# Sums of squares by head of the first attention, from high and low parts

## The reference, cut to what matters

```python
q = l2_norm(q) * (A_HEAD_DIM ** -0.5)      # x * rsqrt(sum(x*x, -1) + EPS), 16 heads of 128
k = l2_norm(k)
...
lower = where(tri_strict, einsum('bhncd,bhnsd->bhncs', k_beta, k) * decay, 0.0)
sol = triangular_solve(eye + lower, rhs)
qk = einsum('bhncd,bhnsd->bhncs', q, k) * decay
...
o = rms_norm_2(o, out_norm_w)              # over the 128 channels of a head
```

## Time and profile before

| what | us |
|---|---|
| median of 3 runs | 1421.38 (1419.54 to 1422.17) |
| the profiled execution's own time | 1419.68 |
| its span in the trace | 1417.9 |
| PE busy | 1391.6 (98%) |
| weight loads busy | 1186.7 (84%) |
| DVE busy | 974.6 (69%) |
| ACT busy | 763.8 (54%) |
| POOL busy | 142.5 (10%) |

### The profile page before, as it was taken

How to read it: one execution, slowest core, us unless ns; L and a number is a source line. 1 busy time by engine, 2 the same in 40 slices (tenths; PEclk the granted TensorE clock), 3 DMA queues, 4 the chain that set the end, 5 groups by cost and what they waited for, 6 DMA issues and landing times.

```text
span 1417.9 us, 20634 instructions
## 1 busy us (share of the span) xinstructions
PE 1391.6 (98%) x7982; PEld 1186.7 (84%) x7982; DVE 974.6 (69%) x1199; ACT 763.8 (54%) x923; POOL 142.5 (10%) x148
## 2 busy tenths in 40 slices
PE   6999999999999999999899999999999999999998
PEld 2446999888888888888799988888888888888887
DVE  3748999876678787789856748746655666656552
ACT  2215435455686677743456665546556566556431
POOL 0000011000060321011234300000000000000000
PEclk9999999999999999999999999999999999999999
DMA  9998899764365445463544566544545555555552
GB/s 385 417 412 349 332 409 409 250 204 152 134 238 192 157 171 182 161 215 136 184 160 144 183 196 215 183 169 171 201 148 188 184 178 178 180 176 179 177 188 81
DMA packets 78295, 303.72 MB, mean 214 GB/s; under 512 B 8768, under 2 KB 8896, under 8 KB 73728
## 3 DMA queue, kind: packets, MB, share of 16 engines
q1 hardware_dynamic: 67680, 261.30, 51.8%
q0 software_dynamic: 10528, 41.19, 8.2%
HBM read 291.97 MB, written 12.58 MB: 215 GB/s over the span
## 4 chain that ended last, share of the span: by engine, by line
PE 87%; DVE 7%; DMA 2%; ACT 2%; issue 1%; SPq 1%; DVEq 0%
PE acc L729 36%; PE acc L731 18%; PE misc L756 3%; PE acc L756 3%; DVE w_lo L1579 3%; PE misc L985 2%; PE acc L687 2%; PE acc L688 2%; PE acc L689 2%; PE acc L679 2%; PE acc L678 2%; PE acc L676 2%; DMA mod_ring<-mod_w 1%; PE misc L880 1%; PE misc L679 1%
## 5 line engine op out<-in xcount | busy, mean ns | idle before, releaser
L1579 DVE TENSOR_TENSOR w_lo<-raw,w_hi 128x1024 fp32r<-128x1024 f32 x392 | 478.1, 1239 | 247.2 <-ACT w_hi L1151 242.5
L729 PE MATMUL acc<-b_op,w_hi 128*128 128x512 f32 x1792 | 635.1, 398 | 2.6 <-DVE vo L1617 2.3
L1151 ACT ACTIVATE w_hi<-raw 128x1024 fp32r<-128x1024 f32 x392 | 405.7, 1054 | 262.5 <-PE acc L731 145.8
L731 PE MATMUL acc<-b_op,w_lo 128*128 128x256 f32 x1792 | 499.4, 279 | 0.0
L729 PEld LDWEIGHTS acc<-b_op,w_hi 128*128 128x128 f32 x1792 | 336.3, 188 | 79.6 <-DVE vo L1617 2.6
L731 PEld LDWEIGHTS acc<-b_op,w_lo 128*128 128x128 f32 x1792 | 337.6, 188 | 0.5
L729 PE MATMUL acc<-a_op,w_hi 128*128 128x512 f32 x768 | 269.0, 396 | 0.5 <-DVEq L1968 0.5
L731 PE MATMUL acc<-a_op,w_lo 128*128 128x256 f32 x768 | 213.7, 278 | 0.0
L729 PEld LDWEIGHTS acc<-a_op,w_hi 128*128 128x128 f32 x768 | 144.1, 188 | 34.9 <-DVEq L1968 0.8
L731 PEld LDWEIGHTS acc<-a_op,w_lo 128*128 128x128 f32 x768 | 144.5, 188 | 0.1
L1549 DVE CUSTOM_DVE_ANT_0 mod_ring<-mod_ring,silu_b,vecs 128x2048 f32<-128x2048 f32 x26 | 61.1, 2351 | 46.9 <-DMA mod_ring<-mod_w 46.7
(11 more groups left out here) (251 smaller groups left out, 1845.3 us busy)
## 6 DMA issues: line engine op xcount, KB each, us to landing
raw<-weights SPq DMA_DIRECT2D x392, 512.0 KB, 4.2
mod_ring<-mod_w SPq DMA_DIRECT2D x26, 1024.0 KB, 12.7
u_ring<-weights SPq DMA_DIRECT2D x32, 512.0 KB, 13.0
gate_ring<-weights POOLq DMA_DIRECT2D x30, 512.0 KB, 8.4
mod_late<-mod_w SPq DMA_DIRECT2D x6, 1024.0 KB, 6.3
xres<-x_t SPq DMA_DIRECT2D x4, 512.0 KB, 15.5
xres<-x_t POOLq DMA_DIRECT2D x4, 512.0 KB, 8.6
x_d<-xres POOLq DMA_DIRECT2D x1, 2048.0 KB, 9.1
```

The source lines that it names most:

```text
L729: nc.tensor.matmul(to, w_hi[:, slot, ch], op[:, kt], start=kt == 0, stop=False, skip_group_check=True)
L731: last = nc.tensor.matmul(to[:, 0:T], w_lo[:, slot, ch], op[:, kt, 0:T], start=False, stop=kt == KT - 1, skip_group_check=True)
L1151: nc.scalar.activation(w_hi[:, m.c % HL_SLOTS], raw[:, q.c % RAW_SLOTS], ACT.Copy).then_inc(own.up(s_hi), 1)
L1579: nc.vector.tensor_tensor(w_lo[:, slot], raw[:, q.c % RAW_SLOTS], w_hi[:, slot].bitcast(F32), ALU.subtract).then_inc(own.up(s_lo), 1)
```

## The change

Eleven of the twelve calls of `head_sums` (all but the last sum of o) become sums from two fp32r parts.

- ACT: `norm_inputs` gets a copy of the squares in t2 to `qk_hi` behind the square; behind the squares of o in t4, for j = 0 to 2, there is a copy to `o_hi[j]`. Both raise `s_heads_hi`. The copy of ones to `ones_r` moves from behind the first attention to the start of its loop.
- DVE: `heads_low(n, lo, src, hi)` waits for `s_heads_hi`, subtracts in place (the low part lies where the squares were) and raises `s_heads_lo`. For the query sums it stands behind `query_products` and ahead of `lo_parts(n + 2, 2)`, in round 0 behind these; for the key sums between the first and the second of five `lo_parts`; for o behind the second slab of a group's eight.
- PE: `qk_sums(c)` and `o_sums(j)` wait for `s_heads_lo` and run `sums_of_parts`, two fp32r matmuls a head, at the places where `head_sums` was called.

```diff
--- before.py
+++ after.py
@@ -241,6 +241,7 @@
         t0_at = top[0]
         t0 = at("t0", [P, 8 * REACH], F32)
         t1 = at("t1", [P, 4 * T], F32)
+        t2_at = top[0]
         t2 = at("t2", [P, 4 * T], F32)
         t34_at = top[0]
         t3 = at("t3", [P, 4 * T], F32)
@@ -309,6 +310,10 @@
         sq_hi = at("sq_hi", [P, 4 * T], F32R, vo_at)
         sq_lo = at("sq_lo", [P, 4 * T], F32R, vo_at + 16 * T)
         v_n = at("v_n", [P, 2, GC], F32, vo_at + 8 * PAIRS)
+        t2_lo = at("t2_lo", [P, 4 * T], F32R, t2_at)
+        t4_lo = at("t4_lo", [P, 4 * T], F32R, t34_at + 16 * T)
+        qk_hi = at("qk_hi", [P, 4 * T], F32R, vo_at + 32 * T)
+        o_hi = [at(f"o_hi{j}", [P, 4 * T], F32R, a_at + o) for j, o in enumerate((8192, 8192, 16384))]
         k_s = at("k_s", [P, 4 * T], F32, vo_at + 32 * T)
         acc = ctx.enter_context(nc.psum_tensor("acc", [P, 2, 4 * T], F32))
         misc = ctx.enter_context(nc.psum_tensor("misc", [P, 2048], F32))
@@ -431,6 +436,8 @@
         s_zs = sem("s_zs")
 
         s_ones = sem("s_ones")
+        s_heads_hi = sem("s_heads_hi")
+        s_heads_lo = sem("s_heads_lo")
         s_sqh = sem("s_sqh")
         s_sql = sem("s_sql")
         s_bx = sem("s_bx")
@@ -892,21 +899,35 @@
                                             start=True, stop=True)
                 last.then_inc(s_nrm, 1)
 
+            def sums_of_parts(hi, lo, at_):
+
+                for h in range(BATCH):
+                    out, of = misc[:, at_ + h * T:at_ + (h + 1) * T], slice(h * T, (h + 1) * T)
+                    nc.tensor.matmul(out, ones_r[:], hi[:, of], start=True, stop=False)
+                    last = nc.tensor.matmul(out, ones_r[:], lo[:, of], start=False, stop=True)
+                last.then_inc(s_nrm, 1)
+
             def split_sums(n):
 
+                pe.wait_ge(s_sql, n.v)
+                sums_of_parts(sq_hi, sq_lo, 0)
+
+            def qk_sums(c):
+
                 pe.wait_ge(s_ones, 1)
-                pe.wait_ge(s_sql, n.v)
-                for h in range(BATCH):
-                    out, of = misc[:, h * T:(h + 1) * T], slice(h * T, (h + 1) * T)
-                    nc.tensor.matmul(out, ones_r[:], sq_hi[:, of], start=True, stop=False)
-                    last = nc.tensor.matmul(out, ones_r[:], sq_lo[:, of], start=False, stop=True)
-                last.then_inc(s_nrm, 1)
+                pe.wait_ge(s_heads_lo, c + 1)
+                sums_of_parts(qk_hi, t2_lo, 0)
+
+            def o_sums(j):
+
+                pe.wait_ge(s_heads_lo, 9 + j)
+                sums_of_parts(o_hi[j], t4_lo, 1024)
 
             def query_sums(i):
 
                 if i:
                     pe.wait_ge(s_a, i)
-                head_sums(Num(2 * i + 1), t2)
+                qk_sums(2 * i)
 
             def log_decays(i):
 
@@ -967,7 +988,7 @@
                     fill[2] = lambda: key_query(i - 1)
                 joined(g, b_op, fillers=fill)
                 joined(g + 1, b_op, fillers={
-                    3: lambda: head_sums(Num(2 * i + 2), t2), 6: lambda: key_key(i)})
+                    3: lambda: qk_sums(2 * i + 1), 6: lambda: key_key(i)})
 
             for k in range(9, 12):
                 joined(G_A + k, b_op, fillers={2: lambda: key_query(3)} if k == 9 else None)
@@ -1044,7 +1065,7 @@
             for j in range(4):
                 fill = {s: (lambda s=s: solve(j, s)) for s in range(8)}
                 if j:
-                    fill[4] = lambda: (solve(j, 4), head_sums(Num(8 + j), t4, 1024))
+                    fill[4] = lambda: (solve(j, 4), o_sums(j - 1))
                 joined(G_A + 12 + j, b_op, fillers=fill)
 
             def early_sums_b():
@@ -1332,6 +1353,8 @@
                 nc.scalar.activation(t1[:, 0:4 * T], t0[:, 0:4 * T], ACT.Silu).then_inc(own.up(s_act), 1)
                 act.wait_ge(*own.last())
                 nc.scalar.activation(t2[:, 0:4 * T], t1[:, 0:4 * T], ACT.Square).then_inc(own.up(s_sq2), 1)
+                act.wait_ge(*own.last())
+                nc.scalar.activation(qk_hi[:], t2[:, 0:4 * T], ACT.Copy).then_inc(own.up(s_heads_hi), 1)
 
             def roots_of_sums(c, power):
 
@@ -1348,6 +1371,7 @@
                         at_ = 8 * i + 4 * half
                         nc.scalar.activation(l_c[q, at_:at_ + 4], of, ACT.Copy).then_inc(own.up(s_lc), 1)
 
+            nc.scalar.activation(ones_r[:], ones, ACT.Copy).then_inc(own.up(s_ones), 1)
             for i in range(4):
                 g = G_A + 2 * i
                 n = slab_of(Num(g)) + AHEAD
@@ -1422,6 +1446,9 @@
                 low_half(g, 1)
                 if j >= 0:
                     nc.scalar.activation(t4[:], wide(vo, BATCH * j), ACT.Square).then_inc(own.up(s_sq2), 1)
+                    if j < 3:
+                        act.wait_ge(*own.last())
+                        nc.scalar.activation(o_hi[j][:], t4[:], ACT.Copy).then_inc(own.up(s_heads_hi), 1)
                 if g == G_A + 10:
                     first_tap_v(0)
                 for k in range(8):
@@ -1453,7 +1480,6 @@
                 if g >= G_A + 11 and g < G_AOUT - 1:
                     solve_copies(j + 1, 7)
 
-            nc.scalar.activation(ones_r[:], ones, ACT.Copy).then_inc(own.up(s_ones), 1)
             for j in range(4):
 
                 act.wait_ge(s_x1, 4 + j + 1)
@@ -1856,6 +1882,12 @@
                 of_k = s_scaled_k if c in (1, 3, 5, 7) else None
                 evicted_half(G_A + c, h, r2[:], (s_scaled if c < 12 else s_zr) if h else of_k)
 
+            def heads_low(n, lo, src, hi):
+
+                dve.wait_ge(s_heads_hi, n)
+                nc.vector.tensor_tensor(lo[:], src[:, 0:4 * T], hi[:].bitcast(F32), ALU.subtract
+                                        ).then_inc(own.up(s_heads_lo), 1)
+
             def normed_heads(c, out):
 
                 dve.wait_ge(s_rinv, c + 1)
@@ -1886,7 +1918,10 @@
                 lo_parts(n + 1, 1)
                 if i:
                     query_products(i - 1)
+                    heads_low(2 * i + 1, t2_lo, t2, qk_hi)
                 lo_parts(n + 2, 2)
+                if i == 0:
+                    heads_low(1, t2_lo, t2, qk_hi)
                 evicted(2 * i + 1, 0)
                 lo_parts(n + 4, 2)
                 taps(2 * i + 1, t0, t4, range(0, 2))
@@ -1899,7 +1934,9 @@
                 taps(2 * i + 1, t0, t4, range(2, 4))
                 if i == 3:
                     identity_blocks()
-                lo_parts(n + 1, 5)
+                lo_parts(n + 1, 1)
+                heads_low(2 * i + 2, t2_lo, t2, qk_hi)
+                lo_parts(n + 2, 4)
                 normed_heads(2 * i + 1, k_n)
                 evicted(2 * i + 2, 0)
                 lo_parts(n + 6, 1)
@@ -1983,6 +2020,8 @@
                 for k in range(8):
                     if g >= G_A + 11 and g < G_AOUT - 1 and k:
                         solve_updates(j + 1, k - 1)
+                    if 0 <= j < 3 and k == 1:
+                        heads_low(9 + j, t4_lo, t4, o_hi[j])
                     if g == G_A + 8 and k == 3:
                         query_products(3)
                     if g in ROWS:
```

## The result

| what | before | after |
|---|---|---|
| median of 8 runs each, us | 1421.49 (1418.72 to 1422.94) | 1426.55 (1424.75 to 1428.17) |
| ratio of the medians, 95% interval | | 1.0037 (1.0027 to 1.0047) |
| profiled execution, us | 1419.68 | 1425.01 |
| its span, us | 1417.9 | 1423.2 |

The change makes the kernel slower by 5.1 us, 0.37%; run a second time, it was again slower, at 1.0028 (1.0017 to 1.0040) of the time before. The forecast was 1427.4 us.

A forecast was written before the change was run, and what follows sets the result against it. PE is 98% busy, but the loop is as long through ACT and DVE; 11.6 us added less 5.5 taken up, taken as 6.0, puts the span at 1423.9, the profiled execution at 1425.7, the median at 1427.4 us (range 1421.0 to 1431.5).

The forecast's parts named there:

- Zero lead at three places: At log_decays, key_key and step 6 of the solve PE has next to no lead; its 8.5 us saving costed at zero.
- A split call is 0.77 us cheaper: Eleven sum calls on PE take 1.19 instead of 1.96 us each, 8.5 us of PE saved in all.
- rival E: The split sums are no cheaper on PE; the forecast would stand; no chance of its own.
- Query sums: 1.8 us on DVE and ACT, less a transfer wait: Before log_decays: eviction and first_tap move 1.8 us, 1.10 taken up in round 1, root 0.7 later; 3.4 taken up over four rounds.
- Key sums: 1.1 us, less a wait for PE: Before key_key: the copy adds 1.1 us a round, less the third hi_parts' waits for PE, 2.1 us over four rounds.
- The sum of the loop: 4 x (1.8 + 1.1) = 11.6, less 5.5 of waits taken up: 6.1, taken as 6.0 us later at the last key_key.
- One sign of the list: Expected in the new trace: the distance from one key_key to the next grows by 1.1 to 1.7 us.
- Sums of o: nothing: Second stage: copy and subtraction fall in waits, 0.1 us each at most; step 6 waits 0.43 + 0.77 = 1.2 us.
- A: PE's time is what counts, waits at the three places not real: 8.5 us faster, 1412.9 us; chance 0.11.
- B: Copies and subtractions all hidden in waits, savings stay lost: same time, 1420.5 to 1424 us; chance 0.12.
- C: Raw transfers behind the delayed lo_parts keep their wait: 9.0 us instead of 6.0, 1430.4 us; chance 0.17.
- D: PE's clock falls at a new log_decays wait, once each round: 14.2 us in all, 1435.6 us; chance 0.03.

The follow-up runs named there:

- the saving without the work: Against the kernel before: ACT's square written rounded, no copy or subtraction, PE runs two fp32r matmuls a head, low part left out; 1421.60 us, ratio 0.9996.
- plain sums in the new order: Kernel before, sums plain, ACT's and DVE's order changed so the query and key roots and k_n come earlier, o's root behind its hi_parts; 1419.78 us, ratio 0.9980.
- the fastest kernel: Reordered changed kernel with one early hi_parts of round 0 moved behind norm_inputs and DVE's order fitted; 1414.03 us, ratio 0.9947 to the kernel before.
- split sums in the new order: Changed kernel with ACT's and DVE's order altered for earlier query and key roots: 1415.03 us, ratio 0.9947 to the kernel before; the second is the fastest kernel.

## Why the prediction held, step by step

**Zero lead at three places.** Right. Taking 0.7 to 0.8 us from PE ahead of each brought waits of about that size and no time (the saving without the work: in round 1 0.97 and 0.89, at step 6 1.17 us of idle at the weight loads, time 0.9996). Working out each place from when the answer is ready against when PE asks for it was the step that decided the sign; the busy shares said the opposite. The Trainium skill (Perfetto Trace Analysis, section Identifying the Most-Contended Engine) says to optimize the engine with the highest occupancy first, and to judge TensorE's headroom by the busy share of its weight loads instead. By either share PE comes first here, at 98% and 84%, and some 8 us less of its work gave 0.1. The question to put beside the shares is whether a chain through other engines is as long.

**A split call is 0.77 us cheaper.** Right for the four query calls (1.18 us each), a little too large for the other seven, which take 1.25 to 1.27: 0.69 to 0.78 us a call, about 8 us in all for 8.5. The query call of round 1 after, first and last matmul and the second regular one behind them:

```profile
453.68 0.28 PE L906 MATMUL misc<-qk_hi,ones_r 128*128 128x256 f32 x1
...
454.51 0.28 PE L907 MATMUL misc<-t_lo,ones_r 128*128 128x256 f32 x1
...
454.86 0.28 PE L738 MATMUL acc<-b_op,w_lo 128*128 128x256 f32 x1
```

454.86 - 453.68 = 1.18 us, for 1.96. So rival E was not the case.

**Query sums: 1.8 us on DVE and ACT, less a transfer wait.** Right in every link, and 0.14 us too large at the end. ACT and DVE of round 1 after, mixed in order of time:

```profile
446.63 1.06 ACT L1355 ACTIVATE t<-t 128x1024 f32<-128x1024 f32 x1
...
447.72 1.06 ACT L1357 ACTIVATE qk_hi<-t 128x1024 fp32r<-128x1024 f32 x1
...
448.82 1.23 DVE L1888 TENSOR_TENSOR t_lo<-t,qk_hi 128x1024 fp32r<-128x1024 f32 x1 [0.57 <-ACT qk_hi L1357]
...
452.34 0.69 DVE L1643 TENSOR_TENSOR t<-acc,t 128x512 f32<-128x512 f32 x1
...
453.80 0.91 ACT L1345 ACTIVATE t<-t,vecs 128x256 f32<-128x256 f32 x2 [3.58 <-DVE t L1645]
...
454.61 1.99 ACT L1172 ACTIVATE w_hi<-raw 128x1024 fp32r<-128x1024 f32 x2
...
460.35 1.15 ACT L1192 ACTIVATE t<-t,small 128x1024 f32<-128x1024 f32 x1
```

DVE waits 0.57 us for the copy (0.6 forecast), subtracts, and its eviction starts at 452.34; before it was 449.88. Counted from the key_key ahead, which is itself 0.67 us later, that is 1.79 us (1.8 forecast). first_tap waits for it, and the two hi_parts behind it are one row without a wait for a transfer: the 1.10 us is taken up. That holds in all rounds; the view of waits between 390 and 612 us (engine, line, what for: us, times, longest) has no row of ACT waiting for raw, where it was 3.4 us:

```profile
DVE t_lo L1888 <- ACT qk_hi L1357: 9.6, 8, 2.2
...
ACT w_hi L1172 <- PE acc L738: 6.4, 7, 1.1
...
PEld misc L887 <- ACT t L1192: 6.3, 4, 1.7
...
PEld misc L887 <- DVE k_n L1629: 3.4, 4, 0.9
```

The root ends at 461.50, 1.23 later than before, 0.56 counted from that key_key; 0.7 was forecast. The difference is an overlap: two hi_parts with no wait between them take 1.99 us, not 2 x 1.06. Before, they took 3.21 us, from 452.15 to 455.36, with 1.10 of waiting in it. So 1.22 us went, 0.12 more than the wait itself, which is nearly the 0.14 missing.

**Key sums: 1.1 us, less a wait for PE.** Right, and again 0.1 us too large. Round 1:

```profile
474.43 1.06 ACT L1357 ACTIVATE qk_hi<-t 128x1024 fp32r<-128x1024 f32 x1
...
475.39 2.94 ACT L1172 ACTIVATE w_hi<-raw 128x1024 fp32r<-128x1024 f32 x3
...
476.89 0.36 PE L906 MATMUL misc<-qk_hi,ones_r 128*128 128x256 f32 x1 [0.46 <-DVE t_lo L1888]
...
482.07 1.06 ACT L1192 ACTIVATE t<-t 128x1024 f32<-128x1024 f32 x1
...
485.74 1.22 DVE L1629 TENSOR_TENSOR k_n<-t,t 128x1024 f32<-128x1024 f32 x1
```

The three hi_parts take 2.94 us with no wait, and the 0.23 us that the third had waited is gone. k_n ends at 486.96. That is 1.99 us later than before (484.97), where the query root was 1.23 later: this part adds 0.76 us, and I had 1.1 - 0.23 = 0.87. The overlap is the difference again (2.94 for three rows of 1.06). PE waits 0.46 us at the sums themselves, inside the longer wait at key_key, as forecast.

**The sum of the loop.** 5.30 us against 6.0, the mis-sized term: by rounds 1.65, 1.31, 1.33 and 1.01, where the working gives 1.72, 1.57, 1.69 and 1.06. All four are over, by 0.05 to 0.36. In round 1 the 0.26 is the two overlaps just shown, 0.12 and 0.11, and rounding: durations of single rows were added where rows of one engine overlap by about 0.1 us. For the others I haven't taken it apart. One sign of the list was missed by this: the distance from one key_key to the next grew by 1.31, 1.33 and 1.01 us, where 1.1 to 1.7 was put down. The forecast is 0.85 us above the median measured, and this is nearly all of it. The parts in runs of their own, 3.18 and 1.88 us for the query and key sums, stand against 4 x 1.8 - 3.4 = 3.8 and 4 x 1.1 - 2.1 = 2.3: the first is off by 0.6, the second by 0.4.

**Sums of o: nothing.** Right: 137.88 us from end to end of that part, for 137.87, and the kernel with only these sums split is at 1.0000. Step 6 waits 1.17 us, the 0.43 of before and 0.74 more; two of the three:

```profile
758.82 0.97 PEld L1051 LDWEIGHTS misc<-vo,t 128*128 128x128 f32 x8 [1.17 <-DVE vo L1629]
...
798.39 0.97 PEld L1051 LDWEIGHTS misc<-vo,t 128*128 128x128 f32 x8 [1.18 <-DVE vo L1629]
```

One row was not as forecast. Two of the three subtractions took nearly twice the 1.2 us put down; one of these and the one that didn't, each with the GpSimd instruction nearest to it:

```profile
730.51 3.52 POOL L631 TENSOR_TENSOR t<-l_x,consts 128x512 f32<-128x512 f32 x2 [1.24 <-PE misc L1006]
...
732.80 2.30 DVE L1888 TENSOR_TENSOR t_lo<-t,o_hi 128x1024 fp32r<-128x1024 f32 x1
...
770.13 2.55 POOL L631 TENSOR_TENSOR t<-l_x,consts 128x512 f32<-128x512 f32 x2
...
773.70 1.21 DVE L1888 TENSOR_TENSOR t_lo<-t,o_hi 128x1024 fp32r<-128x1024 f32 x1
```

The slow one begins while GpSimd multiplies (730.51 to 734.03), the other 1.0 us behind such a multiplication's end (772.68). Seven profiles have these subtractions, 21 in all: each of the 14 that took 2.3 us overlaps such an instruction of GpSimd, and none of the 7 that took 1.2 does. So a DVE subtraction beside GpSimd's work cost 1.1 us more. No run changes GpSimd's order to test that. It cost nothing here, as the 137.88 us show.

**The rivals.** A is out by the saving without the work. B, nearly all hidden, is out: it ended at a loss of 2.6 us, and the loop lost 5.30 and 5.71 us in the two profiles. C, a transfer that lands later by as much as it is issued later, is out: the wait is gone in all four rounds. It was the right question to ask: when the subtraction goes behind the eviction the wait is back at 0.75 us, so this transfer does bind as soon as ACT is less late. D, a clock that falls at the new waits, is out as well. The windows behind log_decays of round 1 and, for comparison, behind DVE's stretch at the start of the second part, kernel after:

```profile
461.00:466.00 5.00, 4.45 (x29) 4.16 (x30) 3.46 (x4) 3.68 (x6) 0.00 (x0) 1.00 0.54 175
690.00:695.00 5.00, 3.79 (x18) 3.79 (x18) 4.93 (x12) 2.44 (x3) 0.00 (x0) 0.52 0.51 174
```

Behind a wait of 1.53 us the granted clock stays at 1.00 (2.4 GHz); in the other stretch, around a wait of PE of 3.02 us, it is at 0.52.

## What to carry to other kernels

Before an engine's work is made cheaper, work out for each place where it takes something back from another engine how long the answer has been there when it asks; if that is near nothing, the saving is spent waiting there, and any work that the edit puts ahead of the answer is paid, less the waits on its way that it takes up (here 5.3 us of the 11.6 added), however idle the other engines are on average. Such an edit pays only together with an order that brings the answer earlier: here 5.1 us slower alone, 7.1 us faster with it, of which the order with plain sums gives some 2. When waits on an engine go away, add its back-to-back instructions by rows that hold several of them, not by rows of one.

## What the hardware showed that I had not expected

**Where the clock falls differs between executions of the same kernel, and it is worth 2 us.** The stretch from the last key_key to the second part took 104.4 to 104.6 us in four profiles (before, after, plain sums in the new order, and the fastest kernel) and 106.1 to 107.2 us in the other eight, the second profile of the kernel after among them. In its last microseconds PE waits for ACT and DVE ahead of step 1 of the solve (32 small matmuls) and again ahead of step 2 (16 of them). The two steps in the first profile of the kernel after,

```profile
691.21 6.62 PE L1006 MATMUL misc<-t,t 128*128 128x128 f32 x32 [3.02 <-ACT t L1439]
...
701.88 2.05 PE L1006 MATMUL misc<-t,t 128*128 128x128 f32 x16 [1.26 <-DVE t L1629]
```

and in the second profile of the same kernel:

```profile
691.81 3.84 PE L1006 MATMUL misc<-t,t 128*128 128x128 f32 x32 [2.45 <-ACT t L1439]
...
703.02 3.78 PE L1006 MATMUL misc<-t,t 128*128 128x128 f32 x16 [4.59 <-DVE t L1629]
```

In the first the clock has fallen at step 1 (0.52 between 690 and 695 us, shown above), whose matmuls take 6.62 us instead of 3.84, but DVE sets the start of step 2, so it costs nothing (step 2 starts 98.73 us behind the last key_key here and 98.60 in the second profile), and step 2 has the full clock. In the second, step 1 has the full clock and so a longer wait follows, 4.59 us; the clock falls behind that one, as these windows show, and step 2 takes 3.78 us instead of 2.05, with nothing to cover it:

```profile
690.00:695.00 5.00, 3.19 (x28) 3.19 (x29) 4.93 (x10) 3.04 (x3) 0.14 (x1) 1.00 0.65 220
...
700.00:705.00 5.00, 1.98 (x9) 1.99 (x10) 5.00 (x7) 2.19 (x5) 0.00 (x0) 0.59 0.56 203
```

All four short profiles have step 2 at 2.05 us and step 1 at 5.46 to 6.62; all eight long ones have step 2 at 2.80 to 3.79, and seven of them step 1 at 3.84 or 3.85 (the kernel with only the key sums split has 5.47). By these rows 1.73 of the some 2 us are step 2's slower matmuls. Why step 1 meets the fallen clock in one execution and not in another is open: the code is the same. A difference of under 2 us between two single profiles of this kernel says nothing until it is placed.

**115 us of PE's work ran at two speeds.** Behind the second part PE is the bound, and the same 655 matmuls took 114.29 us busy in the kernel before,

```profile
841.00:955.80 114.80, 114.29 (x655) 99.70 (x654) 76.40 (x93) 63.28 (x75) 0.53 (x1) 1.00 0.59 198
```

and 115.57 in the kernel after, both at a clock shown as 1.00:

```profile
845.00:961.00 116.00, 115.57 (x655) 100.36 (x654) 76.50 (x93) 62.97 (x74) 0.90 (x2) 1.00 0.59 195
```

That is 1.1%, and it doesn't go with the change: the profiles of the kernels with only q split and with the saving alone are at the faster speed, that of the plain sums in the new order at the slower one. Further on there is a second difference of this kind, and it goes with two kernels: from the end of the second part to the end of the span ten profiles take 576.7 to 578.2 us, the two of split sums in the new order 581.5 and 580.7, though none of the edits touches what runs there. Over the same groups of PE, from about 193 us behind the second part on, PE is busy for all of 291.0 us in the kernel before and for all of 293.6 in the fastest one, both at a clock shown as 1.00. So 3 to 4 us of what these two win in the loop and the second part (8.9 us in the profile of the fastest) are lost again. I don't know the cause of either.
